# Moving expert rows from VectorE to TensorE in the middle steps of a decoder layer

## What is computed

```
h = rmsnorm(x) * (1 + scale1) + shift1
proj = h @ w_in                     # q, k, v, u, gv, two gates; 1024 columns each
out_b = stick_breaking_attention(q, k, v)      # 8 heads of 128, strictly causal
out_a = u * (w_spatial @ layernorm(gv))        # in chunks of 128 positions
x = x + gate1 * ((gate_a * (out_a @ w_ba) + gate_b * (out_b @ w_bb)) @ w_out)
h2 = rmsnorm(x) * (1 + scale2) + shift2
# experts: 8 heads, each token takes its best 16 of 16384
s = (h2 @ w_query) x sub_keys ; experts, gates = top 16 of pair sums, softmax
coef = gates * gelu(h2 . expert_down[experts])
x = x + gate2 * sum_k coef_k * expert_up[experts_k]
y = rmsnorm(x) * g_final
```

## Time and profile before

| | |
|---|---|
| three runs | 2390.11, 2391.7, 2401.53 us; median 2391.7 |
| the profiled execution | 2380.01 us, span 2377.8 us |
| TensorE matmul | 1856.2 us busy, 78% of the span |
| VectorE | 1558.0 us, 66% |
| GpSimd | 1263.7 us, 53% |
| ScalarE | 559.9 us, 24% |
| DMA | 844.90 MB, mean 355 GB/s |
| gathers (queue q0) | 604.05 MB, 65.7% of 16 engines' span |
| mean granted clock of TensorE | 0.876 |

### The profile page before, as it was taken

How to read it: one execution, slowest core, us unless ns; L and a number is a source line. 1 busy time by engine, 2 the same in 40 slices (tenths; PEclk the granted TensorE clock), 3 DMA queues, 4 the chain that set the end, 5 groups by cost and what they waited for, 6 DMA issues and landing times.

```text
span 2377.8 us, 24899 instructions
## 1 busy us (share of the span) xinstructions
PE 1856.2 (78%) x7896; PEld 1296.7 (55%) x7896; DVE 1558.0 (66%) x3451; ACT 559.9 (24%) x1186; POOL 1263.7 (53%) x1169
## 2 busy tenths in 40 slices
PE   4785879888898786998977999778466567777777
PEld 2555878676777564765754577666344223222232
DVE  1210155778888667776787876767679987676662
ACT  1040021476211122136322310111111212122121
POOL 0000025656665455664676665655467677767773
PEclk7997979888999887999977876989688899999999
DMA  7875879998999889996999999999899999999997
GB/s 265 343 274 161 296 292 362 410 348 291 353 388 410 327 324 364 410 412 250 386 408 409 380 401 361 401 380 351 294 410 333 356 358 410 392 409 409 409 409 268
DMA packets 219009, 844.90 MB, mean 355 GB/s; under 512 B 26495, under 2 KB 35639, under 8 KB 197376
## 3 DMA queue, kind: packets, MB, share of 16 engines
q0 software_dynamic: 165888, 604.05, 65.7%
q1 hardware_dynamic: 36820, 216.87, 24.0%
q10 hardware_dynamic: 16172, 22.39, 2.7%
HBM read 826.16 MB, written 16.80 MB: 355 GB/s over the span
## 4 chain that ended last, share of the span: by engine, by line
PE 38%; DMA 21%; DVE 17%; POOL 7%; issue 7%; DVEq 5%; ACT 3%; SPq 1%; ACTq 0%; POOLq 0%
PE bank L846 11%; DMA gather_ring<-in_expert_down,expert_numbers 9%; PE bank L837 9%; PE bank L1202 7%; DVE gather_ring L1920 4%; DVE expert_sums L1951 4%; DMA gather_ring<-in_expert_up,expert_numbers 4%; DMA weight_chunks<-in_w_in 3%; POOL gather_ring L802 3%; POOL gather_ring L787 3%; PE bank L1126 2%; SPq L693 1%; PE bank L1123 1%; DMA weight_chunks<-in_w_ada 1%; POOL weight_chunks L787 1%
## 5 line engine op out<-in xcount | busy, mean ns | idle before, releaser
L787 POOL DMA_INDIRECT gather_ring<-in_expert_down,expert_numbers x510 | 590.0, 1157 | 778.1 <-DVEq L1883 363.3
L1202 PE MATMUL bank<-gather_ring,coef_diagonals 128*128 128x512 f32 x1040 | 578.7, 698 | 264.6 <-DMA gather_ring<-in_expert_up,expert_numbers 155.9
L802 POOL DMA_INDIRECT gather_ring<-in_expert_up,expert_numbers x532 | 564.0, 1060 | 274.1 <-issue 135.1
L1920 DVE CUSTOM_DVE_ANT_0 gather_ring<-gather_ring,h_tiles 128x1024 f32<-128x1024 f32 x410 | 500.1, 1226 | 187.1 <-DMA gather_ring<-in_expert_down,expert_numbers 167.5
L1202 PEld LDWEIGHTS bank<-gather_ring,coef_diagonals 128*128 128x128 f32 x1040 | 213.8, 219 | 561.3 <-issue 402.1
L846 PE MATMUL bank<-hT,weight_chunks 128*128 128x128 f32 (+2 forms) x2304 | 412.4, 341 | 30.4 <-DVE u_and_gv L1773 9.8
L846 PEld LDWEIGHTS bank<-hT,weight_chunks 128*128 128x128 f32 x2304 | 382.0, 202 | 79.8 <-issue 48.8
L1951 DVE SCALAR_TENSOR_TENSOR expert_sums<-gather_ring,expert_coefs,expert_sums 128x1024 f32<-128x1024 f32 x269 | 345.8, 1285 | 8.6 <-issue 8.6
L837 PE MATMUL bank<-weight_chunks,hT 128*128 128x256 f32 x960 | 219.3, 387 | 18.7 <-DMA weight_chunks<-in_w_in 18.2
L837 PEld LDWEIGHTS bank<-weight_chunks,hT 128*128 128x128 f32 x960 | 185.4, 195 | 54.6 <-DMA weight_chunks<-in_w_in 22.7
L1512 ACT ACTIVATE coef_diagonals<-identity,expert_coefs 128x128 f32<-128x128 f32 x304 | 108.3, 395 | 375.4 <-DVE expert_coefs L1931 178.6
(11 more groups left out here) (266 smaller groups left out, 2055.2 us busy)
## 6 DMA issues: line engine op xcount, KB each, us to landing
weight_chunks<-in_w_in SPq DMA_DIRECT2D x84, 1024.0 KB
weight_chunks<-in_w_ada SPq DMA_DIRECT2D x24, 1024.0 KB
weight_chunks<-in_w_query SPq DMA_DIRECT2D x24, 1024.0 KB
weight_chunks<-in_w_branch_a SPq DMA_DIRECT2D x12, 1024.0 KB
weight_chunks<-in_w_branch_b SPq DMA_DIRECT2D x12, 1024.0 KB
weight_chunks<-in_w_out SPq DMA_DIRECT2D x12, 1024.0 KB
gather_ring<-in_expert_up,expert_numbers POOLq DMA_INDIRECT x532, 11.0
weight_chunks<-in_cache_k SPq DMA_DIRECT2D x16, 512.0 KB
```

Of the source, the lines that this page charges most:

```text
L787: pool.indirect_dma_start(out=d_row(slot), out_offset=None, in_=down, in_offset=bass.IndirectOffsetOnAxis(ap=expert[:, t, h * TOPK + k:h * ...
L802: pool.indirect_dma_start(out=u_row(slot), out_offset=None, in_=up, in_offset=bass.IndirectOffsetOnAxis(ap=expert[:, t, h * TOPK + k:h * T ...
L1202: mm = nc.tensor.matmul(bank[6 + half], diag[:, n % 8, :], u_row(slot)[:, half * 512:(half + 1) * 512], start=(u == PE_TILE[t][0]), stop=( ...
L1920: nc.vector.tensor_tensor_reduce(out=row, in0=row, in1=x, scale=1.0, scalar=0.0, op0=ALU.mult, op1=ALU.add, accum_out=dots[:, m % 2, k:k + ...
```

## The change

One line, the table of numbers. TensorE takes 4 rows of 16 in steps 4 to 7, where it took none in 4 and 5 and 8 in 6 and 7, and 10 in steps 8 to 23, where it took 6. VectorE adds the rest.

```
-PE_SHARE = [0] * 6 + [8] * 2 + [6] * 16 + [TOPK] * 12
+PE_SHARE = [0, 0, 0, 0] + [4] * 4 + [10] * 16 + [TOPK] * 12
```

## The result

The changed kernel takes 2416.57 us (median of 7 runs, 2409.45 to 2425.89) beside 2392.83 us for the kernel before on the same chip (7 runs, 2387.05 to 2401.6): a ratio of 1.0097, 95% interval 1.007 to 1.0124. It is slower, by 23.7 us between the medians. The forecast was +16 us, 2408, in a range of 2366 to 2438.

What follows compares the result with a forecast made beforehand. No engine bounds the whole: stretches wait for TensorE, VectorE, full DMA queues or a mix. Terms 6.9 + 15.5 + 7.0 - 10.3 - 3.0 = +16 us on the median 2391.7 gave 2408 us, range 2366 to 2438.

Steps and rivals of the forecast that it cites:

- Past values, +15.5: 1342 to 1463 us, TensorE alone the chain: 9 rows more at 1.72 us, +15.5 us, upper bound +30.
- fourth rival: TensorE holds the up slots, stalling GpSimd's gathers and VectorE: wait for L1202 74.4 to 124 us, +50, 2442 us; chance 0.12.
- Last steps, -10.3: 1754 to 1862.4 us, VectorE first in the chain: 8 adds fewer, -10.3 us, bounded at -5 and -10.3.
- Steps 4 and 5, 0: 646.8 to 774.4 us, DMA share 1.01: 8 more rows on TensorE cost 0, between -10 and +14 us.
- Steps 6 and 7, -3.0: 774.4 to 914.2 us: 8 rows fewer on TensorE, -4.9, adds back on VectorE, +1.9, together -3.0 us.
- Project, +6.9: 979.3 to 1040.8 us, TensorE alone the chain: 4 rows more at 1.72 us, none hidden, +6.9 us.
- the mark of 3 to 4 us more a step: Sign of being right: same project pieces 3 to 4 us longer a step, TensorE at 100%, lower DMA share.
- Merge, +7.0: Merge, output and query, 1463 to 1754 us, mixed chain: 17 rows change sides, +7.0 us, bounds -6.7 and +13.7.
- Steps 10 to 14, 0: Attention, gates and past scores, 1040.8 to 1342 us: added rows hidden, 0; +26 us if none hidden beside gates and past scores.
- The first rival: Gathers decide over steps 8 to 23, DMA share 0.96, so nothing changes: 2392 us; chance 0.28.
- the second: VectorE sets the pace; 64 adds leave it in steps 8 to 23, -20 us, 2371 us; chance 0.14.
- the third: Clock rises to 0.90 in the past values, -13 us there in place of +15.5, 2379 us; chance 0.09.

Runs made afterwards that it cites:

- e3_past: Kernel before with 10 rows on TensorE (6 before) in steps 15, 16 and 17 alone: 2410.27 us, ratio 1.0086.
- e4_last: Kernel before with 10 rows on TensorE (6 before) in steps 22 and 23 alone: 2376.73 us, ratio 0.9932.
- e6_steeper: Kernel before, TensorE rows 4 in steps 6, 7, 9, 10, 12, 15, 18; 2 in 16; 0 in 17; 10 in 19; 13 in 22, 23: 2373.86 us.

## Why the prediction was right, and where its terms were not

The direction and the range held: slower by 24 us between the medians, 8 more than forecast. That the sum came so near is in good part luck, since the largest loss of the early steps was forecast at nothing and two other terms were too high. The reason given, that TensorE is the chain in places and VectorE only at the end, is what e3_past and e4_last show. By its terms:

- **Past values, +15.5: right by its price.** Steps 16 and 17 ran 9 rows more (22.75 for 13.75, four records of L1202 a row) and took 14.1 us more than in the two profiles of before, 1.6 us a row for the 1.72 forecast. In the six other profiles with 6 rows the two steps took 128.1 to 131.6 us for 126.0 and 126.5, so the rows' price can be as low as 1 us. Step 15 lies half in the stretch before, which I priced at 0, and half in this one; three more rows ran in it. Its +12.5 is against the short length that both profiles of before happened to have: four profiles with 6 rows have the long one, and by the estimate above the change adds 2 to 3 us there on average. The term counted rows by their duration and left out that a row behind the exponents holds GpSimd's queue, the down gathers and so VectorE. That is the fourth rival's mechanism, at one place, and it works under both tables.
- **Last steps, -10.3: right.** -9.4 in the profiles, and -8.1 alone (the median of e4_last, -14, is more than that). What is late next are the gathers, as named: the DMA share went from 0.92 to 1.00.
- **Steps 4 and 5, 0: wrong, the worst-sized term.** +12.6, near its upper end of +14, which is the 8 rows' own duration. "The queues are full" was taken for "nothing else is the chain". But the kernel before has L846 35.2% and L1951 15.3% of the chain in that stretch, a row that the prediction left out; TensorE had 16.8 us of idle time, but not where the rows went.
- **Steps 6 and 7, -3.0:** -5.5, and with the later steps left as before -7 to -8. The sign was right.
- **Project, +6.9:** +2.0 in step 9 and about +2.3 in step 10. The step has 33 records of L1202 for 26, so not quite two rows more, and 186 of L837 for 196: part of the projection ran in the neighbouring steps. TensorE is 98% busy there, as forecast; the rows of a stretch cut at a fixed time were not the rows that the step gained, and the mark of 3 to 4 us more a step was missed.
- **Merge, +7.0:** -2.2, inside its bounds of -6.7 to +13.7 but with the other sign. Step 18 lost some 4 us and step 19 won 5 to 8.
- **Steps 10 to 14, 0:** +7.3, most of it in steps 10 and 12, where TensorE's idle time fell from 9 us a step to 4. I gave +26 if none of the rows beside gates and past scores were hidden; most were.

The errors went both ways, and the sum of +16 was nearer than its parts. The forecast's own range, 2394 to 2429, counts both upper bounds but only the merge's lower one; with the -10 of steps 4 and 5 it would begin at 2384. The marks that I had set: 9 and 16 grew and 13 and 14 hardly did, the last steps lost 5 us each, the clock in the past values stayed under 0.85 (0.75). L1202's share was to be 12% and is 18.4%, and L1951's under 4%, which it is. GpSimd's wait for L1202 passed the 110 us named for the fourth rival (134.8 us for the 124 worked out), but it cost a fraction of the 50 us: GpSimd's wait for VectorE fell by 42 us meanwhile, so most of the new wait took the place of an old one (31 of 56 us in the second profiles). That was one of my marks of being wrong, and it was set too low. The fourth rival's mechanism is seen in step 15, and there the wait is as long, 21 to 25 us, in four profiles with 6 rows. The first rival, the gathers, is out by the interval; the second holds in steps 22 and 23 only, as e4_last shows; the third is out, with a clock of 0.75 in the past values and those steps longer.

## What to carry to other kernels

When work can go to either of two engines, give each stretch its own share: the same four rows gain 4 us in a step that waits for VectorE and cost 4 to 10 where TensorE is the chain, and only the chain of that very stretch says which it is; a DMA share of 1.0 does not. Look also at what stands ahead of the moved piece in its new engine's order, since a buffer that it holds can stall a queue that has nothing to do with either engine. Before a profile is used as the base of a forecast, compare its time with the median: this one lay 12 us below, and one step that comes in two lengths, 12 us apart, had the short one in it.

## What the runs showed of the hardware

- The same instructions in the same order (the kernel before and e4_last up to there) had a granted clock of 1.00 in one execution and 0.67 in another over the first 10 us of step 15, and the step took 49 or 62 us; in the runs with 6 rows the clock at its head and its length went together. The Trainium skill (TensorE: Matmul & The Clock Gate, What's actually happening) says that the gate's decisions are not tied to the program's start, so that a kernel can meet them at another point from run to run. The two executions agree with it: they come apart in the clock while TensorE does the same work without a wait. In step 15 that was 12 us of some 2390.
- Taking rows off TensorE lowered its clock: 0.63 and 0.66 in step 17 with 0 and 2 rows for 0.72 with 6, 0.56 in step 16 of e6_steeper with 2 for 0.61 to 0.69 with 6, while 10 rows raised it to 0.77 in step 17. A part of what a row costs comes back in the matmuls around it: in step 17 of the changed kernel the rows take 14.4 us more and the other matmuls 4.5 less.
- The add's two inputs from SBUF: by the rule of the Trainium skill that the prediction named (SBUF — State Buffer, Who interferes with whom), 64 adds fewer were to speed GpSimd up by an estimated 15 us. L787 did fall, from 297.5 us for 254 gathers to 280.6 for 255, but L802 rose from 277.1 to 293.9 for 255 each. Together they stayed at 574.6 and 574.5 us (577.7 and 573.7 in the second profiles): here little or nothing came of it.

The rows of these gathers, steps 8 to 23 of the changed kernel:

```profile
L802 POOL DMA_INDIRECT gather_ring<-in_expert_up,expert_numbers x255 | 293.9, 1153 | 205.4 <-PE bank L1202 134.8 <-issue 68.8 <-DVE expert_sums L1951 1.8
L787 POOL DMA_INDIRECT gather_ring<-in_expert_down,expert_numbers x255 | 280.6, 1101 | 195.7 <-DVE expert_dots L1920 121.1 <-issue 66.2 <-DVEq L1883 8.4
```
